# A two-block network on one core: query tiles before the last state outputs, query norms beside the state projection, and a feed-forward tile begun inside another

## The reference, cut to what matters

```python
def conv_ffn(x, w_in, conv_w, conv_b, w_out):          # first block, second half of each layer
    h = depthwise_conv3(x @ w_in) + conv_b              # 2 x 2816 channels
    u, g = jnp.split(h, 2, axis=-1)
    return (jax.nn.silu(g) * u) @ w_out                 # 2816 -> 1024

# second block
z = rmsnorm(x) @ w_in
q, k, v, f, u_ssm, g_attn, g_ssm = split(z)
q, k = rmsnorm(q per head), rmsnorm(k per head)         # 8 heads of 64
y_attn = softmax(q k^T / 8 + F[t] - F[s], causal) v     # F: running sum of log sigmoid(f)
# state space: 32 groups of 16 channels, 64 complex states each
state[t] = A_bar * state[t-1] + B_bar u[t];  y = Re(C state) + D u
y = gelu(y);  y_ssm = y * sigmoid(y @ w_glu)
mixed = sigmoid(g_attn) * (y_attn @ w_proj_attn) + sigmoid(g_ssm) * (y_ssm @ w_proj_ssm)
x = x + mixed @ w_out;  x = x + moe(rmsnorm(x))         # 32 experts, top 2 in the top group
```

## Time and profile before

| | us |
|---|---|
| median of three runs | 2160.73 |
| the profiled execution | 2161.81 |
| its span | 2160.1 |
| PE busy | 1956.3 (91%) |
| DVE busy | 1284.1 (59%) |
| mean granted TensorE clock | 0.962 of 2.4 GHz |

### The profile page before, as it was taken

The page is one execution under the profiler, slowest core; times in us unless marked ns, Lnnn a source line. Parts: engine busy times, 40 slices in busy tenths (PEclk is TensorE's granted clock), DMA queues, the critical chain, the costliest instruction groups (busy, mean ns, idle before and its releaser), DMA issues.

```text
span 2160.1 us, 25861 instructions
## 1 busy us (share of the span) xinstructions
PE 1956.3 (91%) x8906; PEld 1371.1 (63%) x8907; DVE 1284.1 (59%) x2046; ACT 756.3 (35%) x1282; POOL 776.2 (36%) x1237
## 2 busy tenths in 40 slices
PE   7998889999998998988999999799898897987885
PEld 5873468888786884466888878567665476332332
DVE  7567666678645547477668844799936784111113
ACT  4256733344322336644334422322133631110000
POOL 0325766666301004776666600075602020111100
PEclk9999999999999999999999999899999997999998
DMA  4210123233223210121333222233311064799994
GB/s 158 88 62 29 50 94 106 105 103 117 82 94 141 81 69 40 67 80 69 117 108 107 99 94 100 98 128 107 117 59 59 25 268 176 313 424 423 424 377 181
DMA packets 44698, 293.71 MB, mean 136 GB/s; under 512 B 8188, under 2 KB 8444, under 8 KB 21424
## 3 DMA queue, kind: packets, MB, share of 16 engines
q1 hardware_dynamic: 32544, 253.30, 31.3%
q0 software_dynamic: 11040, 27.46, 3.4%
q10 hardware_dynamic: 1008, 11.53, 1.3%
HBM read 279.50 MB, written 25.17 MB: 141 GB/s over the span
## 4 chain that ended last, share of the span: by engine, by line
PE 76%; DVE 10%; DMA 7%; ACT 3%; issue 2%; POOL 1%; SPq 0%; ACTq 0%; DVEq 0%; POOLq 0%
PE bank L887 11%; PE bank L888 11%; PE bank L889 11%; DMA experts<-in_experts 6%; PE bank L1339 4%; PE bank L1077 3%; PE bank L1079 3%; PE bank L1078 3%; PE bank L999 2%; PE bank L1013 2%; PE bank L1095 2%; PE bank L1096 2%; PE bank L1097 2%; PE bank L1368 2%; PE bank L974 1%
## 5 line engine op out<-in xcount | busy, mean ns | idle before, releaser
L887 PE MATMUL bank<-h_high,w_high 128*128 128x512 f32 x1056 | 418.5, 396 | 40.1 <-ACT h_high L1603 13.6
L888 PE MATMUL bank<-h_low,w_high 128*128 128x512 f32 x1056 | 415.8, 394 | 0.0
L889 PE MATMUL bank<-h_high,w_low 128*128 128x512 f32 x1056 | 415.5, 393 | 0.0
L1594 ACT ACTIVATE w_high<-extra 128x2048 fp32r<-128x2048 f32 (+1 forms) x105 | 182.5, 1738 | 331.8 <-DVE w_low L2078 331.7
L2075 DVE TENSOR_SCALAR extra<-ring 128x2048 int32<-128x2048 int32 (+1 forms) x105 | 118.3, 1126 | 251.8 <-PE bank L889 123.0
L887 PEld LDWEIGHTS bank<-h_high,w_high 128*128 128x128 f32 x1056 | 201.7, 191 | 92.3 <-issue 28.5
L889 PEld LDWEIGHTS bank<-h_high,w_low 128*128 128x128 f32 x1056 | 201.2, 191 | 42.4
L888 PEld LDWEIGHTS bank<-h_low,w_high 128*128 128x128 f32 x1056 | 201.6, 191 | 41.6
L2078 DVE TENSOR_TENSOR w_low<-ring,extra 128x2048 fp32r<-128x2048 f32 (+1 forms) x105 | 219.4, 2090 | 3.6
L1339 PE MATMUL bank<-experts,rstd 128*64 128x512 f32 x496 | 141.8, 655 | 30.4 <-DMA experts<-in_experts 21.8
L1078 PE MATMUL bank<-act_low,w_high 128*128 128x512 f32 x352 | 139.2, 396 | 0.0
(11 more groups left out here) (525 smaller groups left out, 4113.2 us busy)
## 6 DMA issues: line engine op xcount, KB each, us to landing
experts<-in_experts SPq DMA_DIRECT2D x29, 2048.0 KB, 31.4
ring<-in_w_ffn_in SPq DMA_DIRECT2D x44, 1024.0 KB, 4.9
experts<-in_experts SPq DMA_DIRECT2D x30, 1024.0 KB, 28.6
ring<-in_w_ffn_out SPq DMA_DIRECT2D x32, 704.0 KB, 4.0
ring<-in_w_feature SPq DMA_DIRECT2D x14, 1024.0 KB, 4.8
last_slot<-in_experts SPq DMA_DIRECT2D x5, 2048.0 KB, 30.6
ring<-in_w_rest SPq DMA_DIRECT2D x9, 1024.0 KB, 4.9
ring<-in_w_out SPq DMA_DIRECT2D x8, 1024.0 KB, 4.9
```

Of the source, the lines that this page charges most:

```text
L887: pe.matmul(dst, high[:, at], h_high[:, k, :], start=p == 0, stop=False)
L888: pe.matmul(dst, high[:, at], h_low[:, k, :], start=False, stop=False)
L889: return pe.matmul(dst, low[:, at], h_high[:, k, :], start=False, stop=p == KD - 1)
L1594: act.activation(w_high[par_][:, 0:words], w_part[par_][:, 0:words], ACT.Copy).then_inc(w_split, 1)
```

## The change

Three places of the order are rewritten.

1. Feed-forward output. A third buffer for high parts is laid over `h_low` and its masked part over `h`, and `OUT_BUFFER` deals the 16 blocks over three buffers. PE takes tile 0 up to hidden tile 18, then the first half of tile 1, then the last three products of tile 0, then the second half of tile 1. DVE and ACT split block 2 between hidden tiles 18 and 19, and block 3 right behind the last hidden tile.
2. State stage. At its start the copies of u 0 and u 1 on ACT come ahead of the first middle block's high part; DVE splits middle block 1 after the first scan instead of ahead of it. At its end q 0 and q 1 are multiplied ahead of the last C products, and f behind these. DVE splits middle block 12 before the last gelu polynomial and block 13 right behind it; ACT copies q 0 and q 1 once POOL has finished its last rotation.
3. The normalisations leave the glu stage; two stand behind each of the eight `pssm` gate products, in the order q 0, k 0, q 1, k 1 and so on. The scores of a pair of heads wait only for their own four.

```diff
+OUT_BUFFER = [n % 3 if n < BLOCKS_FFN_OUT - 2 else n % 2 for n in range(BLOCKS_FFN_OUT)]
+ACTS_FIRST = 19
...
-    out += [(name, m) for m in range(KD) for name in ("ffn_half", "ffn_out")]
+    out += [("ffn_half", 0), ("ffn_half", 1), ("ffn_out", 0), ("ffn_out", 1)]
+    out += [(name, m) for m in range(2, KD) for name in ("ffn_half", "ffn_out")]
...
+        w_part.append(h_flat[:, 0:SLOT])
+        w_high.append(h_low_flat[:, 0:SLOT])
...
+                def ffn_out(m, lo, hi):
+
+                    n = 2 * m + lo // (JF // 2)
+                    high, low = w_high[OUT_BUFFER[n]], w_low[(BLOCK_FFN_OUT + n) % RING]
+                    dst = bank[4 + m % 2][:]
+                    pe.wait_ge(w_split, l * SPLITS + (SPLIT_OUT + n + 1))
+                    for kk in range(lo, hi):
+                        if m == 0:
+                            pe.wait_ge(act_split, l * JF + (kk + 1))
+                        at = slice(kk % (JF // 2) * P, (kk % (JF // 2) + 1) * P)
+                        pe.matmul(dst, high[:, at], act_high[kk], start=kk == 0, stop=False)
+                        pe.matmul(dst, high[:, at], act_low[:, kk, :], start=False, stop=False)
+                        ins = pe.matmul(dst, low[:, at], act_high[kk], start=False, stop=kk == JF - 1)
...
+                ffn_out(0, 0, JF // 2)
+                ffn_out(0, JF // 2, ACTS_FIRST)
+                ffn_out(1, 0, JF // 2)
+                ffn_out(0, ACTS_FIRST, JF)
+                ffn_out(1, JF // 2, JF)
+                for m in range(2, KD):
+                    pe.wait_ge(x_added, l * (2 * KD) + (KD + m - 1))
+                    ffn_out(m, 0, JF // 2)
+                    ffn_out(m, JF // 2, JF)
...
-            state_outputs(ST - 2)
...
             for t in range(8):
                 mid_tile(FIRST_QK + t)
-                if t == 0:
+                if t == 1:
+                    state_outputs(ST - 2)
                     pe.wait_ge(w_split, F_SPLIT)
...
-                        pe.wait_ge(qk_norm, 16)
                         pe.wait_ge(cum_in, 32)
+                    if n % PAIR == 0:
+                        pe.wait_ge(qk_norm, 4 * (n // PAIR + 1))
...
+                def out_high(n):
+                    split_high(SPLIT_OUT + n, OUT_BUFFER[n], words)
+
+                out_high(1)
+                act_high_parts(EARLY, ACTS_FIRST)
+                out_high(2)
+                act_high_parts(ACTS_FIRST, JF - 1)
                 silu(1, l * (2 * JF) + 2 * JF)
                 act_high_parts(JF - 1, JF)
+                out_high(3)
                 act.preload_act_table_set("natural_log_exp_and_others")
...
-            mid_weights(0)
             u_copy(0)
             u_copy(1)
-            mid_weights(1)
+            mid_weights(0)
...
                     u_copy(n)
+                    if n == 2:
+                        mid_weights(1)
...
+            act.wait_ge(rotated, ST)
+            qk_copy(0)
+            qk_copy(1)
             gelu_sigmoid(YT - 1)
+            mid_weights(MID_BLOCKS - 2)
             act.preload_act_table_set("natural_log_exp_and_others")
+            act.wait_ge(pe_done, done2("C", ST - 1))
+            qk_square(0)
+            qk_square(1)
...
                 split_out(1)
-                split_act(EARLY, JF - 1)
+                split_act(EARLY, ACTS_FIRST)
+                split_out(2)
+                split_act(ACTS_FIRST, JF - 1)
                 conv_rest(JF - 1, JF - 1)
                 split_act(JF - 1, JF)
+                dve.wait_ge(pe_done, done(l, "ffn_half", 0))
+                split_out(3)
...
             split_mid(0)
-            split_mid(1)
...
-                elif st in (5, 9, 13):
+                elif st in (1, 5, 9, 13):
                     split_mid(next_mid[0])
...
-            y_poly(YT - 1)
             split_mid(next_mid[0])
             assert next_mid[0] == MID_BLOCKS - 3
+            y_poly(YT - 1)
+            split_mid(MID_BLOCKS - 2)
             y_gelu(YT - 1)
...
             for m_ in range(YT):
-                normalise_qk(m_, 0)
-                normalise_qk(m_, 1)
                 dve.wait_ge(glu_sig, m_ + 1)
...
                 dve.tensor_tensor(gates[:, KD + m_, :], gates[:, KD + m_, :], bank[m_ % 2][:], ALU.mult).then_inc(ssm_mixed, 1)
-                if m_ < 4:
-                    normalise_qk(4 + m_, 0)
-                    normalise_qk(4 + m_, 1)
+                normalise_qk(m_ % 2 * 4 + m_ // 2, 0)
+                normalise_qk(m_ % 2 * 4 + m_ // 2, 1)
```

More of the change, by code:

```diff
@@ L1062, in _ @@
                     ffn_in((BLOCK_FFN_IN + j) % RING, j, j, l * (2 * JF) + (2 * j - 3))
-                for m in range(KD):
-                    if m >= 2:
-                        pe.wait_ge(x_added, l * (2 * KD) + (KD + m - 1))
-                    for b, name in enumerate(("ffn_half", "ffn_out")):
-                        pe.wait_ge(w_split, l * SPLITS + (SPLIT_OUT + 2 * m + b + 1))
-                        low = w_low[(BLOCK_FFN_OUT + 2 * m + b) % RING]
-                        for k in range(JF // 2):
-                            kk = b * (JF // 2) + k
-                            if m == 0:
-                                pe.wait_ge(act_split, l * JF + (kk + 1))
-                            at = slice(k * P, (k + 1) * P)
-                            dst = bank[4 + m % 2][:]
-                            pe.matmul(dst, w_high[b][:, at], act_high[kk], start=kk == 0, stop=False)
-                            pe.matmul(dst, w_high[b][:, at], act_low[:, kk, :], start=False, stop=False)
-                            ins = pe.matmul(dst, low[:, at], act_high[kk], start=False, stop=kk == JF - 1)
-                        finish(ins, name, m)
+                def ffn_out(m, lo, hi):
[10 more added lines that the diff above has]
+                        ins = pe.matmul(dst, low[:, at], act_high[kk], start=False, stop=kk == JF - 1)
+                    if hi == JF // 2:
+                        finish(ins, "ffn_half", m)
+                    elif hi == JF:
+                        finish(ins, "ffn_out", m)
```

60 lines of the change are left out of this document (33 added, 27 removed).

## The result

Three runs of the changed kernel gave 2130.25 to 2131.09 us, median 2130.66, against 2160.73 before: a ratio of 0.9862, 95% interval 0.9848 to 0.9876. The forecast was 2130.5 in a range of 2124.5 to 2141. The profiled execution took 2131.09 us with a span of 2129.4, so its own difference is 30.7 us.

What follows compares the result with a forecast made beforehand. PE bounds the kernel; its idle time at four seams and the half clock behind can be won. 15.7 + 1.3 + 9.1 + 5.6 - 1.5 = 30.2 us off 2160.73 gives 2130.5 us, range 2124.5 to 2141.

Steps and rivals of the forecast that it cites:

- Feed-forward tail: Output projection of both layers: PE's waits and half clock there go, 15.7 us gained (12.8 to 16.8).
- Block 4: Feed-forward tail: this weight block loads in 4.0 us and is split by 589.7, just when PE wants it.
- Head of the state stage: Start of the state stage: u's copy and the scans come earlier, C too; 1.3 us gained (0.4 to 3.2).
- plus half of a slowed stretch of 4.0 to 6.9 us: Second pair's B and gate tile after PE idles 4.6 us: half clock puts C at 1414.3 to 1415.8.
- the rule weighed there: State stage's head: GpSimd shares SBUF interfaces with VectorE and contends with two-SBUF-input instructions; scans 1.2 us later if rotation runs.
- the alternative of 29.0 us: State stage's head: if POOL's rotation slows the second tile's scans, total gain 29.0 us (2131.7) instead of 30.2.
- End of the state stage: q 0 and q 1 fill PE's 7.87 us wait for POOL, C at full clock; 9.1 us gained (7 to 9.6).
- Projection: Gate and state projection: fourth operand 4.5 us earlier, clock 2.0, first maximum 0.9 later; 5.6 us gained (3.6 to 6.5).
- Clock elsewhere: Restarts after the long waits that stay: low-clock stretches can be longer, 1.5 us lost (0 to 4).
- ACT's new queue: Rival, state stage's end: ACT's strict list runs 6 us late and delays the norm sums; about 2143 us, chance 0.15.
- The expert phase moved as a whole: Expert loads follow PE's last tile and start earlier; its rival, the phase swallows the gain, 2160.7 us, chance 0.04.
- none waits for a buffer: Against the rival that three buffers make weights late in later feed-forward tiles, up to 2174 us, chance 0.03.

Runs made afterwards that it cites:

- u_ffn: The changed kernel with the old feed-forward tail (two buffers for high parts, output tile 0 whole before tile 1); 2145.77 us.
- f_inorder: The changed kernel with PE's old order in the feed-forward tail, third buffer and early split of block 2 kept; 2147.73 us.
- h_fill: The changed kernel with 18 unread products ahead of the second pair's B products in the state stage; 2129.33 us.
- f_fill: The changed kernel with the old feed-forward tail, its two waits on PE filled with 11 and 9 unread products; 2141.55 us.
- u_head: The changed kernel with the state stage's head as before (block 0's high part ahead of u's copies, block 1 split ahead of the first scan); 2134.99 us.
- u_end: The changed kernel with the last C products ahead of q 0 again and DVE's and ACT's lists there as before; 2141.63 us.
- u_norm: The changed kernel with q's normalisations back in the glu stage and k's beside the first four gate products; 2137.12 us.
- again: The changed kernel unchanged, timed once more on another chip; 2132.47 us, ratio 0.9861 to the kernel before.
- h_tile: The changed kernel with a third middle tile (g 0) ahead of the second pair's B products and two instead of three behind; 2129.22 us.
- fill_norm: The changed kernel with unread products in PE's seven long waits behind the norms; 2146.22 us.

## Why the prediction was right, and where its terms were not

**Feed-forward tail: right but for block 4, and so 0.5 to 0.7 us a layer too much.** Block 2 has no wait; block 3 is 0.5 us late as foreseen. Block 4 was put at 589.7, just where PE would want it, and came at 590.0: SP starts its load at 581.82, 0.1 us behind the 581.7 of the prediction, and DVE starts on it 4.2 us later, not 4.0. PE was there at 589.6, so a second wait of 0.5 us stands where none was counted. 14.55 us for the two, inside the bounds. u_ffn gives 13.7 from the times, and f_inorder shows that without PE's new order nothing of it comes.

**Head of the state stage: the step that failed is "plus half of a slowed stretch of 4.0 to 6.9 us", as a gain of 1.3.** The places were right: the second scan ends 43.4 us behind "norm" (1404.9 foreseen, 1405.2 in before's time), PE's bracket is 4.71 us (4.6), the rotation is ready at 1413.2 (1413.0). The half clock then lasted 6.8 us, nearly the longest stretch allowed for, and C came at 1416.0, outside the forecast of 1414.3 to 1415.8, with a gain of 0.2 us below the bound of 0.4. h_fill shows that the clock is the whole of it (2.7 us back). Nor was 4.0 to 6.9 us wide enough: with the same instructions in this stage f_inorder has 10.2 us and f_fill 3.4 at this restart. And the base was as uncertain as the forecast: u_head shows the old order 2.8 us slower than before's trace has it.

On the rule weighed there: the first rotation ended at 1388.68 and the second tile's scans began at 1388.69, so they ran apart and took 2.33 us as counted, and the alternative of 29.0 us falls. The case that it is about did not arise. Where the two engines do overlap both pay: DVE's subtraction takes 3.27 us instead of 2.29 (at 1392.70 in before, with POOL idle), POOL's second product 3.35 instead of some 1.3. The rows fit the two taking turns. The subtraction starts at 1381.80, while POOL's first product runs to 1382.91, and ends 2.2 us behind that, at 1385.07; POOL's second product starts at 1382.88 and ends 1.2 us behind that, at 1386.23. The Trainium skill ("GPSIMD Engine Reference", section "8. Key points") has the two engines contend when a DVE instruction has two SBUF inputs, as this subtraction has, and the trace agrees that they do.

**End of the state stage: right.** 9.2 for 9.1. POOL's rotation beside the split took 7.99 us (8.1), C waited some 0.14 us (0.1), f's copy held up the norm sum for 0.35 us (0.5). u_end gives 9.6 from the times.

**Projection: right, 5.4 for 5.6.** The last operand came 4.3 us earlier (4.5), the clock gave 2.0 (2.0), the first maximum lost 0.9 (0.9). u_norm gives 5.1 from the times.

**Clock elsewhere: wrong sign, by chance.** -1.5 was taken, +1.6 came, in attention; again, u_ffn, u_norm, f_inorder, h_tile and h_fill have a low stretch there and 107.5 to 107.9 us (u_end has two and 109.2), after, u_head, f_fill and fill_norm have none and 105.8 to 106.0. This and the overestimates of the tail (1.2 us) and of the head (1.1 us) cancel, which is why the total sits 0.2 us from the forecast: luck, not precision. By five rounds on another chip the change is worth 29.5 us; that it would be 30.2 was not known as well as it looks.

**The rivals.** ACT's new queue cost 0.35 us and not 6. The expert phase moved as a whole (30.65 us). The third to the fourth output tile takes 15.17 us, 66 products at 0.23, and no product of a later tile has a bracket in either layer: none waits for a buffer.

## What to carry to other kernels

When a producer is late at a seam, an earlier split or a third buffer alone only moves the wait; it pays when the consumer has independent work to put in front of it, here the next tile's first half. Price a wait at PE as its idle time plus, where PE sets the pace behind it, some 2 to 3 us of half clock, and give the clock's share its full range, before as well as after: the same order can fall on either side. Before an engine's idle time is filled, ask who else is within a few us of the pace: here DVE waited for PE only 5.6 us in the 155 of the loop (after's waits from 1401.8 to 1556.7), and of the 7.0 us that PE won 4.7 came out.

## What was not expected of the hardware

- The same instructions of a stage meet the half clock differently from execution to execution. Of two restarts 18 us apart before has 6.8 us behind the first and none behind the second, u_head 3.4 and 6.8, worth 2.8 us; behind the one restart of the new order stand 3.4, 6.8 or 10.2 us (f_fill, after, f_inorder), worth 2.8 us too (52.57 to 55.33).
- PE's filling with unread products of 0.23 us kept the granted clock at 1.00 through the waits here: 2.7 us a seam in f_fill, 2.7 us in h_fill.
- A product whose two operands come from the table of constants is recorded as two passes of 0.43 us where one of 0.23 serves the split operands (26 rows for 13 products in fill_norm).
